# Norms of the convolution half beside the gate's projection, the mixer's output products on GpSimd, and an attention that takes its units by turns

## What is computed

```python
proj = rms_norm(h, norm_mix_g) @ w_in                    # a | gate | u, 1024 columns each
c = causal_depthwise_conv(a * sigmoid(gate), conv_w, conv_b)      # 31 taps
c = layer_norm(c, ln_g, ln_b);  yc = c * sigmoid(c)               # silu
# S5: bu = B u, states s[t] = lam_bar * s[t-1] + bu[t] (complex), y = Re(C s) + d * u
z = gelu(y);  ys = z * sigmoid(z @ glu_w)
y = concat(rms_norm(yc, grp_norm_conv_g), rms_norm(ys, grp_norm_ssm_g))
h = h + y @ w_out
# cross-attention, 4 heads of 512
s = q k^T / sqrt(512);  p = softmax(s);  o = p v;  h = h + o @ w_o
```

## Time and profile before

| | us |
|---|---|
| median of 3 runs | 4105.94 (4096.61 to 4108.35) |
| the profiled execution | 4102.64 |
| its span, first to last instruction | 4100.9 |
| PE busy in the span | 3809.6 (93%) |
| DVE, ACT, POOL busy | 2775.6 (68%), 2085.3 (51%), 223.1 (5%) |
| mixer stage to the end of its last skip | about 129 (1757.1 to 1886.0) |
| gelu and gate's projection | about 33 (to 1918.9) |
| group norms | about 35 (to 1953.8) |
| attention stage | about 38 (2343.9 to 2382.1) |

### The profile page before, as it was taken

One profiled execution on the slowest core, in us unless ns is written; L12 is line 12 of the kernel. 1 busy time (PEld: TensorE's weight loads), 2 busy tenths in 40 slices (PEclk: granted clock), 3 DMA queues, 4 the chain that ended last, 5 costly groups with the idle time before them and its releaser, 6 DMA issues. The chain is left out here.

```text
span 4100.9 us, 66412 instructions
## 1 busy us (share of the span) xinstructions
PE 3809.6 (93%) x22156; PEld 3150.1 (77%) x22156; DVE 2775.6 (68%) x5248; ACT 2085.3 (51%) x3899; POOL 223.1 (5%) x281
## 2 busy tenths in 40 slices
PE   7899997889999998986899998999979999999998
PEld 1567765768888887854788787888768888888887
DVE  3554346778886667796865565788686676666667
ACT  1443333456665554574454444555585555555554
POOL 4011100000000000021100000000000000000000
PEclk9999998989999999998999998999999999999999
DMA  9787660346676664521555444666517766666655
GB/s 356 289 297 252 251 218 1 119 151 215 214 213 191 188 187 149 176 94 52 167 178 179 154 144 141 217 207 212 163 36 222 222 207 189 189 187 189 189 185 162
DMA packets 204817, 753.75 MB, mean 184 GB/s; under 512 B 23859, under 2 KB 23892, under 8 KB 202708
## 3 DMA queue, kind: packets, MB, share of 16 engines
q1 hardware_dynamic: 176020, 647.07, 49.7%
q0 software_dynamic: 27168, 98.93, 6.6%
q10 hardware_dynamic: 1440, 5.24, 0.3%
HBM read 725.99 MB, written 25.17 MB: 183 GB/s over the span
## 5 line engine op out<-in xcount | busy, mean ns | idle before, releaser
L207 DVE TENSOR_TENSOR weights_lo<-ring,weights_hi 128x512 fp32r<-128x512 f32 x2240 | 1526.5, 696 | 958.7 <-ACT weights_hi L200 947.1
L200 ACT ACTIVATE weights_hi<-ring 128x512 fp32r<-128x512 f32 x2240 | 1399.0, 631 | 1391.1 <-PE ps L982 1330.3
L982 PE MATMUL ps<-expert_parts,weights_hi 128*128 128x512 f32 x4224 | 1459.6, 394 | 12.5 <-DVE expert_parts L940 7.3
L982 PE MATMUL ps<-expert_parts,weights_lo 128*128 128x256 f32 x4224 | 1141.2, 280 | 0.0
L982 PEld LDWEIGHTS ps<-expert_parts,weights_hi 128*128 128x128 f32 x4224 | 778.8, 189 | 174.7 <-issue 15.1
L982 PEld LDWEIGHTS ps<-expert_parts,weights_lo 128*128 128x128 f32 x4224 | 797.0, 189 | 21.5
L982 PE MATMUL ps<-mlp_parts,weights_hi 128*128 128x512 f32 x1024 | 354.2, 394 | 16.7 <-PEq L740 15.8
L982 PE MATMUL ps<-hidden,weights_hi 128*128 128x512 f32 x1024 | 351.5, 392 | 0.6 <-DVE weights_lo L207 0.6
L982 PE MATMUL ps<-mlp_parts,weights_lo 128*128 128x256 f32 x1024 | 277.1, 281 | 0.0
L982 PE MATMUL ps<-hidden,weights_lo 128*128 128x256 f32 x1024 | 275.9, 280 | 0.0
L982 PE MATMUL ps<-h_parts,weights_hi 128*128 128x512 f32 x704 | 267.1, 407 | 8.0 <-PEq L607 8.0
(11 more groups left out here) (483 smaller groups left out, 4944.2 us busy)
## 6 DMA issues: line engine op xcount, KB each, us to landing
ring<-in_w_mlp SPq DMA_DIRECT2D x256, 512.0 KB, 3.6
ring<-in_w_u SPq DMA_DIRECT2D x256, 512.0 KB, 4.2
ring<-in_w_v_tab SPq DMA_DIRECT2D x256, 512.0 KB, 3.7
ada_ring<-in_w_ada POOLq DMA_DIRECT2D x124, 512.0 KB, 6.1
ring<-in_w_mix SPq DMA_DIRECT2D x88, 512.0 KB, 5.2
ring<-in_w_out SPq DMA_DIRECT2D x64, 512.0 KB, 3.7
ada_ring<-in_w_ada SPq DMA_DIRECT2D x48, 512.0 KB, 7.0
ring<-in_w_in SPq DMA_DIRECT2D x48, 512.0 KB, 4.2
```

The source lines that it names most:

```text
L200: act.activation(core.hi[:, g % SLOTS], core.ring[:, slot, at:at + QUARTER], ACT.Copy).then_inc(core.rounded, 1)
L207: dve.tensor_tensor(core.lo[:, g % SLOTS], core.ring[:, slot, at:at + QUARTER], core.hi[:, g % SLOTS].bitcast(F32), ALU.subtract).then_inc ...
L982: mm = pe.matmul(out, part[:, g % SLOTS, k, :], moving, start=at == 0 and part is core.hi, stop=last and part is core.hi)
```

## The change

What it does, in five parts.

- **Mixer, inputs.** `p1` is gone: the product with the cosine is written back into `bu` in PSUM. The rotation is four instructions of 512 columns in place of two of 1024; its result goes to `bt` for the last two of four groups and stays in PSUM for the first two, whose scans read PSUM. PE writes the next inputs in two halves: those of the last two groups when half of the rotation is done, those of the first two when their scans are done.
- **Mixer, outputs.** Both output products of passes 0 to 6 run on POOL, `v` has two buffers and the trigonometric tables three; the last pass has both on DVE. The skip term comes two passes later.
- **Mixer, end.** The gelu in three pieces, the sum of the convolution over its features, the subtraction of the mean, its square and the square's sum stand at the end of the mixer stage.
- **Gate's projection.** `ConvNorm` hooks into it: root, reciprocal, scaling, silu, square, sum, root, reciprocal and scaling of the convolution half, and square and partial sum of each gated tile. `group_norm_stage` keeps the end of the other half's norm and rounds and splits the convolution half for `mix2_out`, which passes over these two quarters (`ready=2`).
- **Attention.** The transposes of a unit follow the scores two units later, DVE takes maximum, division and copy of different units in one turn, and an output tile waits only for the probabilities of its own head (and for its bank).

The diff, cut to its core:

```diff
@@ Layer, linear_stage
+                    if q < layer.ready:
+                        act.sem_inc(core.source_rounded, 1)
+                        return
...
                     dve.wait_ge(core.source_rounded, layer.A + q + 1)
+                    if q < layer.ready:
+                        dve.sem_inc(core.source_split, 1)
+                        return
@@ local_mixers_stage
             def _(pool):
-                for f in range(HT):
-                    pool.wait_ge(s["out_c"], f + 1)
+                for f in range(HT - 1):
+                    pool.wait_ge(s["scanned"], 2 * f + 2)
                     if f:
                         pool.wait_ge(s["y"], f)
-                    pool.tensor_tensor(os[:], v[:], sin(f), ALU.mult).then_inc(s["out_s"], 1)
+                    pool.tensor_tensor(os[:], v[:, f % 2], sin(f), ALU.mult).then_inc(s["out"], 1)
+                    pool.tensor_tensor(oc[:], v[:, f % 2], cos(f), ALU.mult).then_inc(s["out"], 1)
...
+                y = proj[:, 2 * HT:, :]
+                act.wait_ge(s["skip"], HT - 2)
+                act.activation(y[:, 0:HT - 2, :], y[:, 0:HT - 2, :], ACT.Gelu_apprx_tanh)
...
+                act.wait_ge(s["centred"], 1)
+                act.activation(c[:, :, 0:T], conv[:], ACT.Square).then_inc(squared.sem, 1)
...
-                inputs(0)
+                inputs(0, 2)
+                inputs(0, 0)
                 for f in range(HT):
                     taps(f)
                     if f + 1 < HT:
-                        inputs(f + 1)
+                        inputs(f + 1, 2)
                     fold(f)
+                    if f + 1 < HT:
+                        inputs(f + 1, 0)
                     if f:
                         outputs(f - 1)
+                pe.wait_ge(s["convolved"], HT)
+                channel_sum(5, conv).then_inc(summed.sem, 1)
                 outputs(HT - 1)
+                pe.wait_ge(squared.sem, squared.base + 1)
+                channel_sum(CONV_BANK, c[:, :, 0:T])
...
-                    dve.tensor_tensor(p1[:], bu, cos(f), ALU.mult)
-                    dve.tensor_tensor(p2[:], bu, sin(f), ALU.mult).then_inc(s["turned"], 1)
+                    dve.tensor_tensor(p2[:], bu, sin(f), ALU.mult)
+                    dve.tensor_tensor(bu, bu, cos(f), ALU.mult).then_inc(s["turned"], 1)
                     dve.wait_ge(s["turned"], f + 1)
-                    dve.tensor_tensor(bt[:, :, 0, :], p1[:, :, 0, :], p2[:, :, 1, :], ALU.add)
-                    dve.tensor_tensor(bt[:, :, 1, :], p1[:, :, 1, :], p2[:, :, 0, :], ALU.subtract).then_inc(s["rotated"], 1)
+                    dve.tensor_tensor(bt[:, 2:, 0, :], bu[:, 2:, 0, :], p2[:, 2:, 1, :], ALU.add)
+                    dve.tensor_tensor(bt[:, 2:, 1, :], bu[:, 2:, 1, :], p2[:, 2:, 0, :], ALU.subtract).then_inc(s["rotated"], 1)
+                    dve.tensor_tensor(bu[:, 0:2, 0, :], bu[:, 0:2, 0, :], p2[:, 0:2, 1, :], ALU.add)
+                    dve.tensor_tensor(bu[:, 0:2, 1, :], bu[:, 0:2, 1, :], p2[:, 0:2, 0, :], ALU.subtract).then_inc(s["rotated"], 1)
+                    if f >= 2:
+                        skip(f - 2)
+                        dve.wait_ge(s["out"], 2 * f - 2)
...
-                    dve.tensor_tensor(oc[:], v[:], cos(f), ALU.mult).then_inc(s["out_c"], 1)
+                f = HT - 1
+                dve.tensor_tensor(p2[:], v[:, f % 2], cos(f), ALU.mult).then_inc(s["first_diag"], 1)
+                dve.tensor_tensor(bt[:], v[:, f % 2], sin(f), ALU.mult).then_inc(s["first_diag"], 1)
+                skip(HT - 2)
+                dve.wait_ge(summed.sem, summed.base + 1)
+                dve.scalar_tensor_tensor(conv[:], spread(ps[:, 5, 0:T], 1, HT), -1.0 / (HT * P), conv[:], ALU.mult,
+                                         ALU.add).then_inc(s["centred"], 1)
                 skip(HT - 1)
@@ ConvNorm (new), beside the gate's projection
+    def tensor(self, pe, t):
+        if t == 4:
+            pe.wait_ge(self.done["conv_squared"], 1)
+            self.total(pe, CONV_BANK, self.sq, range(HT)).then_inc(self.core.norm_signals[1].sem, 1)
+        if t >= 2:
+            pe.wait_ge(self.done["ssm_squared"], t - 1)
+            self.total(pe, SSM_BANK, self.y_sq, [t - 2])
+    def scalar(self, act, turns):
+        t = turns[0]
+        if t == 0:
+            self.root(act, CONV_BANK, 0)
+        if 1 <= t < 3:
+            act.wait_ge(self.done["scaled"], t)
+            for k in range(4 * t - 4, 4 * t):
+                ins = act.activation(self.c[:, k, :], self.c[:, k, :], ACT.Silu, bias=self.core.prm["ln_b"][:, k:k + 1])
+            ins.then_inc(self.done["silu"], 1)
+        if t == 3:
+            act.wait_ge(self.done["silu"], 2)
+            act.activation(self.sq, self.c, ACT.Square).then_inc(self.done["conv_squared"], 1)
+        if t == 5:
+            summed = self.core.norm_signals[1]
+            act.wait_ge(summed.sem, summed.base + 1)
+            self.root(act, CONV_BANK, 1)
+        if t >= 1:
+            self.square(act, t - 1)
+    def after_tile(self, dve, t):
+        if t == 0:
+            self.inverse(dve, 0)
+        if t < 2:
+            self.scale(dve, 0, range(4 * t, 4 * t + 4), self.c, "ln_g").then_inc(self.done["scaled"], 1)
+        if t == 5:
+            self.inverse(dve, 1)
+        if 5 <= t < 7:
+            self.scale(dve, 1, range(4 * t - 20, 4 * t - 16), self.h, "grp_conv")
@@ group_norm_stage (new body)
+            norm.square(act, HT - 1)
+            for q in range(2):
+                at = slice(q * QUARTER, (q + 1) * QUARTER)
+                act.activation(parts[:, at, 0, :], h[:, at, :], ACT.Copy).then_inc(norm.done["silu"], 1)
+                if q == 0:
+                    act.wait_ge(summed.sem, summed.base + 1)
+                    norm.root(act, SSM_BANK, 2)
...
+            lo(0)
+            norm.inverse(dve, 2)
+            for t in range(HT):
+                dve.scalar_tensor_tensor(h[:, HT + t, :], norm.y[:, t, :], core.prm["grp_ssm"][:, t:t + 1], norm.std[:, 2, :],
+                                         ALU.mult, ALU.mult)
+            lo(1)
@@ attention_stage
                     mm.then_inc(s["scores"], 1)
-                for n in range(8):
...
+                    if n >= LAG:
+                        turn(n - LAG)
                 for n in range(KD):
                     h = n // 4
-                    pe.wait_ge(s["probs"], 8)
+                    if n < LAG:
+                        turn(8 - LAG + n)
+                    pe.wait_ge(s["probs"], max(n + 1, 2 * h + 2) if n < 8 else 8)
...
+                for n in range(8 + LAG + 1):
+                    if n < 8:
+                        largest(n)
+                    if 1 <= n < 9:
+                        divide(n - 1)
+                    if n >= LAG + 1:
+                        keep(n - LAG - 1)
```

More of the change, by code:

```diff
@@ new lines, in glu_stage, with gate, group_norm_stage, _ @@
+def glu_stage(core, y, parts, next_w, norm):
+    def gate(dve, n, slots):
+        dve.tensor_tensor(y[:, n, :], y[:, n, :], slots[0], ALU.mult).then_inc(norm.gated, 1)
+    linear_stage(core, "glu", [
+        Layer("w_glu", HT, [parts], shape=lambda act, n, slots: act.activation(slots[0], slots[0], ACT.Sigmoid),
+              finish=gate, quarters=2, source=y)], next_w, beside=norm)
+    norm.vector_ready()
+def group_norm_stage(core, norm, h, parts):
+    nc = core.nc
+    _, summed, _, _ = core.norm_signals
+    with nc.Block() as block:
+        @block.tensor
+        def _(pe):
+            for t in range(HT - 2, HT):
+                pe.wait_ge(norm.done["ssm_squared"], t + 1)
+                mm = norm.total(pe, SSM_BANK, norm.y_sq, [t])
+            mm.then_inc(summed.sem, 1)
@@ new lines, in _, with lo @@
+            norm.square(act, HT - 1)
[5 more added lines that the diff above has]
+                    norm.root(act, SSM_BANK, 2)
+        @block.vector
+        def _(dve):
+            def lo(q):
+                at = slice(q * QUARTER, (q + 1) * QUARTER)
+                dve.wait_ge(norm.done["silu"], 3 + q)
+                dve.tensor_tensor(parts[:, at, 1, :], h[:, at, :], parts[:, at, 0, :].bitcast(F32), ALU.subtract)
+            lo(0)
+            norm.inverse(dve, 2)
+            for t in range(HT):
+                dve.scalar_tensor_tensor(h[:, HT + t, :], norm.y[:, t, :], core.prm["grp_ssm"][:, t:t + 1], norm.std[:, 2, :],
+                                         ALU.mult, ALU.mult)
+            lo(1)
@@ L2290, in values_stage @@
+    summed.base += 1
 def values_stage(core, mem, v, next_w):
@@ L2382, in _, with largest @@
             def _(dve):
-                for n in range(8):
+                def largest(n):
                     dve.wait_ge(s["scores"], n + 1)
@@ L2386, in _, with divide @@
                     dve.tensor_scalar(top[:, n:n + 1], top[:, n:n + 1], -scale, None, ALU.mult).then_inc(s["max"], 1)
-                for n in range(8):
+                def divide(n):
                     dve.wait_ge(s["exp"], n + 1)
```

176 lines of the change are left out of this document (81 added, 95 removed).

## The result

The changed kernel takes 4080.3 us, the median of 6 runs (4075.4 to 4087.4), where the kernel before took 4100.4 beside it (6 runs, 4096.6 to 4108.4): a ratio of 0.9946, 95% interval 0.9936 to 0.9955, some 22 us (the medians are 20.1 apart). The profiled execution took 4080.53 us with a span of 4078.7 (before 4102.64 and 4100.9).

The account below looks back on a forecast made before the run. PE, busy 93% of the span, bounds the kernel, DVE the mixer's passes; the change works where PE waits. Savings 15.6 + 0.9 + 2.0 + 6.0 = 24.5 us from 4105.94 give 4081.4, stated as 4081, range 4064 to 4099.

Parts of the forecast that it names:

- Mixer, the passes: Mixer stage: passes shorten from 14.36 to 12.3 us (12.2 to 13.0), so pass 7 starts 15.3 earlier.
- it fits by 0.4 us: Mixer pass: POOL's two products, started some 0.3 after the scans, end before DVE's last two groups' scans, 9.8 after.
- Mixer, the end: From pass 7 to the projection: 26.4 us in place of 26.7, so the projection starts 15.6 earlier (10 to 18).
- Projection: Gate's projection: with nine table loads and the norm's work on ACT, 53 us, 24 more than before (48 to 60).
- Norms: Norm stage: 10.1 us in place of 34.95 (9.5 to 12), 24.9 saved; with the longer projection only 0.9 gained.
- Start of the stage with w_out: PE starts at about 0.4, not waiting 2.5; block ends at the same distance, DVE further on: 2.0 saved (0 to 4).
- Attention: Attention stage: transposes between scores let outputs begin sooner, without the 2.0 cold start: 6.0 us saved (4.5 to 6.8).
- 1: Mixer: POOL's products also hold up scans from PSUM, 14.2 a pass: 4093, or 4097 if no pass shortens; chance 0.09.
- 2: Mixer: writing PSUM in place runs at half rate, 15.5 us a pass: kernel 4106; chance 0.07.
- 3: Table loads: each of five more than before costs twice its 1.28 us, 6.4 in all: kernel 4088; chance 0.04.
- 4: Projection: PE's wait for gated tiles' squares forces strict turns, 95 us in place of 53: kernel 4123; chance 0.05.
- 5: Sigmoid and Silu share a table, the clock stays warm, w_out gains 4: kernel 4073; chance 0.13.

Follow-up runs that it names:

- e4: The changed kernel with Sigmoid in place of Silu in the convolution half's norm (another function, five table loads for nine): median 4076.2 us, projection 49.21.
- e7: The changed kernel with each of PE's sums of a gated tile's squares made one projection tile later: projection 54.94 us, longer by 2.6.
- e5: The changed kernel with Silu made as a product with Sigmoid, DVE multiplying in eight added instructions: median 4074.2 us, projection 50.55.
- e9: The kernel before with the changed mixer passes and attention, gelu and all of the norm left where they were: ratio 0.9944 to the kernel before.
- e12: The changed kernel without POOL's squares of mem and their sum, ones in their place (another function): the stage with w_out 374.60 us, shorter by 14.9.
- e3: The changed kernel with the first two groups also rotated into SBUF, so all eight scans of a pass read SBUF: 4106.9 us beside 4103.7 before.
- e8: As e3, but PE's inputs of the first two groups wait for the rotation alone: passes of 13.74 us, mixer stage 10.5 longer than in the changed kernel.

## Why the prediction was right, point by point

**What bounds.** Right. The passes were DVE's, and with `oc` gone they still are: DVE has next to no idle time in a pass (in pass 2 it stands for POOL while counted as busy).

**Mixer, the passes.** Right but for pass 2. Forecast 90.6 to pass 7, measured 91.4: passes 0 and 1 0.4 shorter than said, passes 3 to 6 0.8 shorter (11.97 to 12.23, not 12.3), pass 2 2.0 longer. The step that failed is "it fits by 0.4 us". POOL begins 0.8 after the scans and not 0.3, so that even in the pass shown it overlaps the scans from `mix_bt` by 0.3. For pass 2 the step took every handover at a warm clock and ACT's gather as on time, and neither held. In e4 and e7, where the same outputs ran warm (1.05 for sixteen), pass 2 is 13.27, and the stage, with the sum below, 115.9: about 1 of the 2 is the clock. The other is PE's wait of 2.14 for ACT's gather, which stands in the warm kernels too (2.14 in e4); that is read from the traces, no run takes it away.

**Mixer, the end.** 27.0 for 26.4: the sum of the squares ran cold, 5.41 where I took 4.8 between 3.7 and 5.8. In e4 and e7 it took 3.72.

**Projection.** 52.35 for 53, with the nine loads. Tile by tile on ACT, to the end of its hook: 11.35, 8.8, 6.35, 5.15, 2.9, 8.0, 5.5 and 4.3, where the sum had 10.7, 8.9, 6.4, 5.3, 3.1, 7.5, 5.5 and 4.3. That the stage is a sum of ACT's instructions and of its waits for DVE is what e4, e5 and e7 bear out.

**Norms.** 10.05 for 10.1. Their net worth, said to be 0.9, is 0 to 3 by e9.

**Start of the stage with w_out.** 0.5 for 2.0. PE did begin 1.9 sooner, as said. The failed step is that the block "ends at the same distance" with DVE further on: POOL's 16.7 us shut DVE out all the same (a rest of 0.69 took 6.79), PE waited 3.38 and 6.85 for it, 10.2 in all where it had waited 8.7 before, and ran at 0.70. e12 gives the price of the lock, some 13.5. DVE's rest, beside POOL's first product (1944.00 to 1951.32):

```profile
1945.08 6.79 DVE L207 TENSOR_TENSOR weights_lo<-ring,weights_hi 128x512 fp32r<-128x512 f32 x1 [0.63 <-ACT weights_hi L200]
```

**Attention.** 4.4 for 6.0. The mechanism and its size were right at equal clock (6.1); what was missed is that the scores may start cold, which took 1.7 back.

**Rivals.** 1, that POOL also locks scans from PSUM: 2.41 beside POOL; e3 and e8 show the lock where both inputs are in SBUF, and there a pass takes 13.7 at best, near the rival's 14.2. 2, half rate in PSUM: 2.28. 3, dearer loads: e4, 0.8 for a load that goes. The Trainium skill (ScalarE: Activation LUTs, What ACT_TABLE_LOAD costs) gives about 2.66 us for a switch. This case doesn't agree: each of the nine loads in the stage took 1.28, none with a gap of its own behind it. 4, the projection in strict turns: PE's wait is there in three tiles, 10.9 us, but e7 takes it away and gains nothing. 5, a shared table: the load at 1890.59 behind a Sigmoid says no; its warm clock came true for the attention alone, in two of eleven kernels with turns.

In sum, misses of 1.4 (mixer), 1.5 (w_out) and 1.6 (attention) stand against 0.8 in the projection and norms and 1.4 in untouched code: 22.2 for 24.5. That the median, 4080.3, came out within 1 us of the forecast is luck: before, measured beside it, was 5.5 below the median that the forecast started from, and this made up for what the change gave less.

## What to carry to other kernels

Work that is put beside a stage is free only if the engine that does it has room there, not if the engine that waited for it has: here PE could have covered the norms and ACT could not, so some 25 us saved in one stage cost 24 or 25 in two others. GpSimd beside VectorE cost nothing here where VectorE had an operand in PSUM, and held it up where both operands were in SBUF; of the mixer's 14.2 us, 10.5 hung on four scans a pass that read PSUM. And a wait taken from TensorE is to be judged with where its idle time goes next: e7 lost 2.6 us by the clock, and e12 won 3.3 by it beyond the waits that it took away.

## What the runs showed of the hardware that was not expected

- VectorE multiplied and added in place in PSUM at the price of SBUF (2.28 for 2048 columns, 0.69 for 512), and scanned out of PSUM at the same 0.6 a row of 256 while GpSimd held up scans out of SBUF: in e8 eight of these took 6.53 in place of 4.8.
- The same score products behind the same pause of 2.85 us ran their first 5.5 us at a granted clock of 0.69 in ten traces and at 1.00 in four, with the length of the stage repeating to 0.01 us within each kind.
- Two identical stages can differ through the clock alone: mixer 118.4 or 115.9, in kernels whose code of that stage is the same.
